# Turned gain columns, a four-head half tile, a shared room, a deeper expert ring and another merge order in a hybrid decoder step

## The reference

```
n1 = RMSNorm(x)*(1+scale1)+shift1 ;  h = n1 @ w_in        (1024 x 8704)
branch A: gated linear recurrence, 4 heads, 128x128 state, chunked; head norm * silu gate -> @ w_branch_a
branch B: dilated sliding-window attention, 3 groups x 4 heads x 128, merged by softmax denominators -> @ w_branch_b
x += gate1 * ((sigmoid(gA)*yA + sigmoid(gB)*yB) @ w_out)
n2 = RMSNorm(x)*(1+scale2)+shift2
PEER: q = n2 @ wq, 8 heads; per head two lists of 128 key scores, top 16 of each, top 16 of the 256 sums
      -> 16 experts of 16384; out += softmax * gelu(n2 . u[e]) * v[e];   x += gate2 * out
```

## Time and profile before

| | us |
|---|---|
| median of three runs | 4417.76 |
| the profiled execution | 4406.08 |
| its span, first to last instruction | 4404.3 |
| TensorE busy | 3094.3 (70%) |
| VectorE busy | 2596.8 (59%) |
| ScalarE busy | 1942.7 (44%) |
| GpSimd busy | 1497.0 (34%) |
| HBM traffic | 1455 MB, 330 GB/s over the span |

### The profile page before, as it was taken

One profiled execution on the slowest core, in us unless ns is written; L12 is line 12 of the kernel. 1 busy time (PEld: TensorE's weight loads), 2 busy tenths in 40 slices (PEclk: granted clock), 3 DMA queues, 4 the chain that ended last, 5 costly groups with the idle time before them and its releaser, 6 DMA issues. The chain is left out here.

```text
span 4404.3 us, 46846 instructions
## 1 busy us (share of the span) xinstructions
PE 3094.3 (70%) x14243; PEld 1672.3 (38%) x14243; DVE 2596.8 (59%) x6557; ACT 1942.7 (44%) x6708; POOL 1497.0 (34%) x1174
## 2 busy tenths in 40 slices
PE   7998868874999998575644686875555555555556
PEld 4677754741543456353432464551111111111111
DVE  2362334376568755684655545557767766766774
ACT  2122431045457844564442225445555545545554
POOL 4544102353322333222221112324444444444443
PEclk8999888977999999666876797886777777877778
DMA  6534244389999999877999888999999999999998
GB/s 259 200 131 138 74 152 168 120 324 356 389 368 367 422 421 405 288 305 291 375 342 364 348 305 312 357 348 383 416 410 420 421 401 413 415 400 413 417 403 336
DMA packets 315488, 1450.91 MB, mean 329 GB/s; under 512 B 44258, under 2 KB 105602, under 8 KB 166883
## 3 DMA queue, kind: packets, MB, share of 16 engines
q0 software_dynamic: 152064, 1107.36, 62.5%
q1 hardware_dynamic: 148802, 333.34, 21.5%
q10 hardware_dynamic: 14368, 7.21, 0.6%
HBM read 1380.40 MB, written 74.57 MB: 330 GB/s over the span
## 5 line engine op out<-in xcount | busy, mean ns | idle before, releaser
L3010 POOL DMA_INDIRECT uv_ring<-in_peer_uv,pick_idx x1024 | 1157.4, 1130 | 2240.9 <-PE expert_acc L3183 1954.4
L3183 PE MATMUL expert_acc<-uv_ring,diag 128*64 128x512 f32 (+1 forms) x3968 | 1102.6, 796 | 720.5 <-ACT diag L3148 689.2
L3106 DVE SCALAR_TENSOR_TENSOR uv_ring<-uv_ring,n_pairs 128x1024 f32<-128x1024 f32 x756 | 924.7, 1235 | 574.8 <-DMA uv_ring<-in_peer_uv,pick_idx 525.9
L3183 PEld LDWEIGHTS expert_acc<-uv_ring,diag 128*64 128x64 f32 (+1 forms) x3968 | 241.2, 155 | 1482.7 <-ACT diag L3148 1050.3
L3135 ACT ACTIVATE gelu_cube<-dots_now 128x2 f32<-128x2 f32 x528 | 105.8, 200 | 1001.8 <-DVE uv_ring L3106 920.2
L3106 DVE SCALAR_TENSOR_TENSOR uv_ring<-uv_ring,n_more 128x1024 f32<-128x1024 f32 x268 | 326.4, 1225 | 216.9 <-DMA uv_ring<-in_peer_uv,pick_idx 209.0
L3143 ACT ACTIVATE pick_weight<-gelu_tanh,pick_share 128x1 f32<-128x1 f32 x1056 | 350.8, 379 | 17.6
L955 PE MATMUL h_acc_q<-in_w_all_q,n_all_q 128*128 128x512 f32 x640 | 283.6, 597 | 0.7 <-issue 0.7
L3138 ACT ACTIVATE gelu_tanh<-gelu_cube,dots_now 128x1 f32<-128x1 f32 x1056 | 253.3, 287 | 16.2
L3140 ACT ACTIVATE pick_share<-dots_now,pick_prob 128x1 f32<-128x1 f32 x1056 | 245.4, 280 | 0.0
L952 PE MATMUL h_acc_q<-n_all_q,in_w_all_q 128*128 128x272 f32 x896 | 215.3, 398 | 10.2 <-DMA in_w_all_q<-in_w_in 10.2
(11 more groups left out here) (460 smaller groups left out, 4959.4 us busy)
## 6 DMA issues: line engine op xcount, KB each, us to landing
in_w_p<-in_w_in SPq DMA_DIRECT2D x34, 1024.0 KB, 7.3
in_w_all_q<-in_w_in SPq DMA_DIRECT2D x17, 2048.0 KB
ada_w<-in_w_ada SPq DMA_DIRECT2D x10, 2048.0 KB, 7.9
uv_ring<-in_peer_uv,pick_idx POOLq DMA_INDIRECT x1024
past_keys_q<-in_past_keys SPq DMA_DIRECT2D x16, 1024.0 KB
past_rows_q<-in_past_values SPq DMA_DIRECT2D x16, 1024.0 KB
score_pair<-scores SPq DMA_DIRECT2D x66, 128.0 KB
wq_raw_p<-in_peer_wq SPq DMA_DIRECT2D x16, 512.0 KB, 5.9
```

Of the source, the lines that this page charges most:

```text
L3010: pool.indirect_dma_start(self.rows_of(part, s), None, self.x["peer_uv"][0], bass.IndirectOffsetOnAxis(ap=self.idx[:, q % 2, 2 * half + s, ...
L3106: ins = dve.scalar_tensor_tensor(out=row, in0=row, scalar=1.0, in1=n2[:, s if tile < LAST_TILE else 0, :], op0=ALU.mult, op1=ALU.mult, acc ...
L3183: ins = pe.matmul(self.acc[s * w:(s + 1) * w, c, :], self.diag[:, of % DIAGS, t, 0:w], rows, start=first, stop=last)
```

## The change

Seven parts. (1) Opening: the norm weight and two bias rows come as 24 rows of 128 from ScalarE's queue and TensorE turns them, instead of three loads of single elements on SP's queue; the two first bias loads move to ScalarE's queue; the first projection weights are loaded ahead of the fourth adaLN block; four of the eight columns are scaled and split before the last gains. (2) SP's wait for the last weights at the end of the first projection moves to GpSimd's turn that uses them. (3) First half: four of eight `w_branch_a` products are computed in `merge_phase` into PSUM of their own. (4) Heads 4 to 7 of tile 0 become a four-head group (parts 32 to 63); its search is dealt three steps a turn over turns 22 to 29. (5) Second half: `SharedRoom` takes the sixth ring slot's room after part 119 and holds the inputs of recurrence and attention; the first loads of the next phase are issued in the phase before it, the last stores are waited for in the phase after it. Attention and sample updates get another order. (6) Merge, second half: three spread buffers, of which only the used part is cleared, filled two ahead; the tile merge goes into the middle of the sample steps. (7) The ring has seven slots from part 226 and ten from part 261.

```diff
         modulation.load(2)
+        in_weights.load(0)
         modulation.load(3)
-        modulation.load_bias(0)
-        modulation.load_bias(1)
-        with nc.allow_non_contiguous_dma("one weight and two biases for each column"):
-            sp.dma_start(weight_col[:], x["norm1_w"].rearrange("a (c p) -> p (a c)", p=P)).then_inc(weight_in, 16)
-            for j in range(2):
-                sp.dma_start(bias_cols[:, j, :], x["b_ada"][:, j * D:(j + 1) * D].rearrange("a (c p) -> p (a c)", p=P)).then_inc(weight_in, 16)
-        in_weights.load(0)
...
+        by_chunk = lambda row: row.rearrange("a (c p) -> (a c) p", p=P)
+        act.dma_start(gain_rows[0:DC, :], by_chunk(x["norm1_w"])).then_inc(weight_in, 16)
+        for j in range(2):
+            act.dma_start(gain_rows[(1 + j) * DC:(2 + j) * DC, :], by_chunk(x["b_ada"][:, j * D:(j + 1) * D])).then_inc(weight_in, 16)
+        for b in range(MOD_SLOTS):
+            modulation.load_bias(b, act)
         act.wait_ge(c_loaded, 32)
...
         for c in range(DC):
+            if c == HALF:
+                modulation.copy(MOD_FIRST - 1)
...
-            turn(n)
-            if n + 1 < MOD_FIRST:
-                modulation.product(n + 1)
-            fold(n)
+            if n == N - 1:
+                turn(n)
+                fold(n - 1)
+            modulation.product(n)
+            if n < N - 1:
+                turn(n)
+            if n != N - 2:
+                fold(n)
...
         gains(0)
         modulation.rows(2)
+        for c in range(HALF):
+            move(c)
         gains(1)
-        for c in range(DC):
-            dve.wait_ge(moved, c + 1)
...
 
 class OutWeights:
@@ -699,7 +736,7 @@
 
...
+        else:
+            pool.wait_ge(self.loaded_before[half], 16 * (self.before + k + 1))
...
+            if room is not None and n == len(blocks) - 1:
+                for s in range(SLOTS):
+                    sp.wait_ge(stored[s], stores_in(s, -(-(first[IN_QK // WB] - s) // SLOTS)))
+                beside.wait_summed(MORE_TO + 1)
+                room.gates_and_rows()
...
-            for half in range(2):
-                sp.wait_ge(raw_in[half], 16 * LOADED)
         for s in range(SLOTS):
...
+                room.first_queries()
+                sp.wait_ge(tile_done, N_P)
+                room.first_values()
             beside.sp(cost(n) * (0.2 if w == S_TOK else 0.4))
...
-            sp.wait_ge(state_stored[0], 16 * DEC_B // 2)
-            sp.wait_ge(state_stored[1], 16 * DEC_B // 2)
-            sp.wait_ge(final_stored, 16)
+            sp.dma_start(new_state_p[0, 0].rearrange("h k v -> k h v"), state[:, 0]).then_inc(room.final_stored, 16)
 
...
-                at_least(dve, update_s, b - 1)
-                nc.vector.tensor_scalar(v_one[b % 2], v_in[0:S_TOK, s, :], own_row[:, b:b + 1], None, ALU.mult).then_inc(s_ones, 1)
+                own_values(b + 1)
                 dve.wait_ge(update_s, b + 1)
-                at_least(dve, state_stored[b % 2], 16 * (b // 2))
...
+                if b < HEADS:
+                    sample_rows(b)
...
+            if s == 0:
+                sp.dma_start(self.reset, self.consts["chunk_reset"]).then_inc(self.tables_in, 16)
+                sp.dma_start(self.causal.rearrange("p a b -> p (a b)"), self.consts["chunk_causal"]).then_inc(self.tables_in, 16)
+            sp.dma_start(self.v_in[:, s], self.dram["h_r"][at:at + P, R_I:R_I + WIDTH]).then_inc(self.row_in[s], 16)
+            sp.dma_start(self.g_in[:, s], of_gate(T_G, at)).then_inc(self.row_in[s], 16)
+        sp.dma_start(self.masks.rearrange("p a b -> p (a b)"), self.consts["att_masks"]).then_inc(self.masks_in, 16)
+
...
-            load_keys(j + 2)
-            for i in of_job(j):
-                load_past(i + 2)
             sp.wait_ge(result_ready, j + 1)
             for at, dst in queries(dram["att"][g]):
                 sp.dma_start(dst, result[at, j % 2].rearrange("p h d -> p (h d)")).then_inc(stored[j % 2], 16)
             load_values(j + 2)
+            load_keys(j + 3)
+            for i in of_job(j):
+                load_past(i + 2)
             beside.sp(12.0)
...
+            at_least(dve, added, i - P_SLOTS + 1)
+            if i < P_SLOTS:
+                s_link(nc.vector.memset(p_one[i], 0.0))
+            else:
+                s_link(nc.vector.memset(spread(p_one[i % P_SLOTS], loads[i - P_SLOTS][1]), 0.0))
...
                 for i in range(n * PER, (n + 1) * PER):
-                    spread_probs(i)
+                    if i + P_SLOTS - 1 < len(loads):
+                        spread_probs(i + P_SLOTS - 1)
+                    if i % PER == PER // 2 - 1:
+                        merge(n + 1)
+                    if i % PER == PER // 2 and n:
+                        leave(n - 1)
...
+            if early is not None:
+                early.product(n)
             pe.wait_ge(merged_ready, n + 1)
...
             for j, o in enumerate((o_a, o_b)):
+                if j == 0 and m < begun:
+                    continue
...
-    HEADS_READ = {2: 4, 13: 6}
+    HEADS_READ = {2: 4, 20: 8}
...
-MORE_FROM, MORE_TO = 33, 125
+MORE_FROM, MORE_TO = 33, 119
+QUERY_FROM, QUERY_SLOTS = 226, 2
+TAIL_SLOTS = 3
 LEAD = 2
...
-AS_WRITTEN = (1,)
+AS_WRITTEN, FIRST_FOUR = (1,), 2
+FOUR_SCORES, FOUR_PICKS, FOUR_STEPS = 20, 22, 3
...
+    if tile == 0:
+        return ((0, 2), (2, 2), (4, 4))
+    return tuple((h, 2) for h in range(0, PH, 2))
+
...
+    tail_from = FRONT_PARTS + LEAD + QUERY_SLOTS
+    out = [(PART_SLOTS, MORE_FROM, MORE_TO)]
+    out += [(first + k, QUERY_FROM, N_PARTS) for k in range(QUERY_SLOTS)]
+    out += [(first + QUERY_SLOTS + k, tail_from, N_PARTS) for k in range(TAIL_SLOTS)]
+    return out
```

More of the change, by code:

```diff
@@ L2360, in query_phase @@
     C_S = 1.5
-    stores = [(4 if at // P in QUAD_TILES else 2) if w == P else 1 for _, w, at in tiles]
+    stores = lambda n, heads: sum(P // row_tokens(tiles[n][2] // P, h) if tiles[n][1] == P else 1 for h in range(heads))
     block = ph.block()
@@ L2976, in sp @@
                     self.load_scores(q, s)
[L2977 to L2978 removed]
+        for n, rows in enumerate(ROW_HALVES):
+            if n and i == rows.first - rows.half - (8 if rows.tile == 0 else 1 if rows.half and n >= ROW_SLOTS else 12):
                 self.load_n2(n)
@@ L3226 @@
 MOD_US = 250.0
-FRONT_PARTS = 257
 FRONT_US = 2140.87
@@ L3334, in front @@
                             if busy:
-                                later[0].more = held(rows, "uv_more", [P, 2, 2 * D])
-                            phase(project_phase, tag, busy, span, second, const, n_hi, n_lo, split_weights, ahead, x, consts, dram)
+                                later[0].more[PART_SLOTS] = room.room
+                            phase(project_phase, tag, busy, span, second, const, n_hi, n_lo, split_weights, ahead, x, consts, dram, room)
                             if busy:
```

413 lines of the change are left out of this document (287 added, 126 removed).

## The result

The changed kernel takes 4377.41 us (median of 5, 4363.64 to 4382.25) against 4417.76 (4412.14 to 4424.89): a ratio of 0.991, 95% interval 0.9893 to 0.9927. That is 40 us less; the forecast was 79 less. The profiled executions, 4375.05 against 4406.08 us, differ by 31.

> The changed kernel once more, as the run beside which the three others stand. All theories: ratio 0.991, between 0.989 and 0.993, stages within 3 us of its first profile, except the first half's, where the granted clock differs from run to run.

The account below looks back on a forecast made before the run. It took engines to bound the first half, TensorE and DMA the second projection, and bytes the experts alone. Terms summed to -87, -79 after bytes given back: 4327 us profiled, 4338 as median, 8-in-10 range 4292 to 4398.

Parts of the forecast that it names:

- opening: Start of the kernel up to the first projection: 6 us less (0 to 10).
- search in the first norm: Second half's first norm: tile 0's search puts more steps on VectorE there, 17 us more.
- second projection (sums, sixth slot): Second half's projection: tile 0's sums 17 us less (29 less to 0), losing the sixth slot earlier 2 more.
- recurrence (start, samples, end): Second recurrence: 14 us less at its start, 8 in its samples, 11 at its end.
- attention (start, order): Second half's attention: 5 us less at its start, 8 less by the order of loads.
- merge: Second half's merge: 6 us less (15 less to 0), with TensorE's wait for spread buffers 50.4 us before.
- seven slots, query: Query stage with seven ring slots: 13 us less (30 less to 0), from fewer waits for gathers.
- ten slots, experts alone: End of the kernel, where only experts run, with ten ring slots: 8 us less (34 less to 0).
- bytes given back: Recurrence to merge: a seventh of the 52 us saved comes back as waits for gathers, turning -87 into -79.
- more than forecast: Rival, chance 0.10: TensorE's 29 us come in full, query fills its 21, loads' order gives 20: -130, 4288 us.
- SP's queue as the place for a rival: Rival, chance 0.04: SP waits for part 119 ahead of the last stores, so the prefetch fails: -37, 4381 us.
- the DMA engines bind from 1095 on: Rival, chance 0.18: first half -18, search +19, sums 0, slot +2, recurrence -33, the rest 0: -30, 4388 us.

Follow-up runs that it names:

- the run without the rows: Changed kernel, but tile 1's second half takes its products with the gate's rows, its own norm rows not loaded (output wrong): 4362.4 us, 0.9871 of the kernel before.
- best5: Changed kernel with second row halves loaded two turns earlier and the room's loads two by two between the last stores: 4363.61 us, 0.9883 of the kernel before.
- the one by pairs: Changed kernel, but tile 0 works all its heads two by two as before, searches at one step a turn: 4376.28 us, 0.9899 of the kernel before.

## Why the forecast was half right

By the profiled executions, forecast and measured:

| step | forecast | measured |
|---|---|---|
| opening | -6 | -8.3 |
| end of the first projection | -7 | -7.2 |
| early branch products | -5 | -5.2 |
| other stages of the first half | +2 | +8.5 |
| search in the first norm | +17 | +17.7 |
| second projection (sums, sixth slot) | -15 | +1.7 |
| recurrence (start, samples, end) | -33 | -25.0 |
| attention (start, order) | -13 | -2.3 |
| merge | -6 | -0.1 |
| seven slots, query | -13 | +0.4 |
| ten slots, experts alone | -8 | -12.6 |
| bytes given back | +8 | (in the rows above) |
| branch, out, second norm | 0 | +1.4 |
| sum | -79 | -31 |

*First half.* The three terms held. The first move's copy took 4.00 us beside the split, as the forecast took it from the earlier trace rows, but the three behind it 0.42 each. GpSimd's last split instruction ran from 36.87 to 41.40: only one move lay beside it, since the weights, and with them the split, came earlier too. So the opening gave 8.3 and not 6. The 8.5 us elsewhere are 2.1 and 2.7 in recurrence and attention, where the granted clock was 0.79 and 0.93 for 0.81 and 0.96 (in later profiles of the same code these stages took 116.8 to 123.9 and 118.0 to 126.6 us, 118.6 and 120.4 before), and 3.6 in the query stage, where 2 were forecast.

*Search and sums.* 17.7 us against 17 forecast for the search. In the projection 15 us were to go and none did, and three sizes are behind it. The sums were taken at 17 us, as TensorE's 29 cut down by the DMA share of 0.99; between parts 32 and 64 they gave 34 (29 in the run without the rows). There the rival *more than forecast* was right: TensorE's time came in full. Two costs were not in the sum at all. The half tile makes five row halves out of three in tiles 0 and 1 (the first expectation above says four), with three row slots: a wait of 18.0 us at part 65, 16 us between parts 64 and 66, and 12 of the stage by the run without these rows. And the prefetch was counted at nothing in the projection: 12.5 us, by the run with the loads moved back. That the stage came out at 689.3 and so near the 687.6 before is luck: 34 won, 16 and 13 lost again, and 6 in pieces that no run takes apart, 2 of them forecast for the sixth slot. I had named SP's queue as the place for a rival (17 + 30 us), but had it wait for part 119. It was the issue of the loads itself, and their bytes.

*Recurrence.* The stage took 221.5 us where 213 were forecast. The start gave 15.4 us for 14 (first scan 13.1 us after the barrier for 28.4), and the end 8.3 for 11 (from the last product of the recurrence at 2015.2 to 2028.8 before, from 2005.6 to 2011.0 now). The samples are what was mis-sized: from the first scan to that product 204.4 us became 203.1, 1.3 us less for the 8 counted. The idle 11.2 us of the earlier trace rows at its end are gone from VectorE, and 17.86 us of TensorE's appear at attention's start, where I had counted 5 less. Taking away the wait, reordering the loads or keeping gathers back moved it again.

*Attention, merge, query.* This is the step that failed most: 32 us counted from idle shares of 0.05 to 0.08 in the earlier trace rows, by which a stage could shrink until its share was 1. They gave 2. The new kernel runs these stages at 0.96, 0.97 and 0.93 in the old length. The waits named in the earlier trace rows shrank as forecast and came back as waits for past values and query weights. What the forecast did not ask is where in the stage the idle share lies. In the attention it is one hole of 10 us, in which no gather is in flight since GpSimd waits for TensorE; the change left it there and made it 14. It can be closed: three versions ran the same stage in 267 to 271 us at a share of 0.99 to 1.00. So the 13 us were to be had, but not by the reordering that was to bring them. In the merge one gap could be named, 14.8 us for expert rows; with it gone the stage took 149.5 us once and 152.3 to 154.7 in five other versions, for 150 forecast. For the query stage no run settles what fills the share.

*Slots.* The two counted together, 21 us, gave 15. Most of it comes one way: two more parts (261 for 259) are fetched when the query stage ends, 10 us at 421 GB/s. The query stage took 269.3 us without the slots and 263.6 to 266.0 with them, so it owes them 3 to 6 us of the 13 forecast, which the rest of the change took back.

The rival *the DMA engines bind from 1095 on* had -30 in the profiled run and 4388; measured -31 and 4377 (the profiled run before was 11.7 under its median, the changed one 2.4 under). Its number is right, its reason is not shown, and that is luck. In the projection its *sums 0* was false (34 us won, as much lost elsewhere in the stage), in the attention the engines did not bind (nearly the same bytes passed in 267 us), and the 12.6 us of the experts alone, which it put at 0, made up for 6 less in the first half and 8 less in the recurrence. The rival *more than forecast* names 12, 8 and 12 us over the forecast's 87, which makes -119 and not -130.

Open: why the hole closes, and the attention takes 267 to 271 us, in three runs that changed only where the room's loads stand. A fourth of that kind, with the loads at the recurrence's start, kept the hole and took 284.3, and all others took 277 to 285. From 28 to 56 us after the stage's start the DMA share is 0.94 to 0.97 in the three and 0.47 to 0.71 in the seventeen other profiles. Fewer gathers in flight at the start was the theory; keeping them back did not bring it. It was not seen again in the combined versions: `best5` has the loads between the stores, leaves the attention as it is, and takes 280.7 us there.

## What to carry to other kernels

A wait with a name in the profile is worth its length only if nothing else is late next: ask for each wait removed which load the freed engine wants next, and when it is issued. A mean DMA share of 0.95 says neither that the stage is bound nor that 5% are free: cut the stage into short windows and look for the hole, and for what the engine that issues the gathers waits for in it. A prefetch has its price where it is issued: count the issuing queue's time and the bytes up to the barrier of the stage that hosts it. When a change adds a user of a small set of buffers (here a fifth row half on three slots), draw up who waits for which buffer at every border. And when a run undoes two things at once, as the one by pairs did, its difference is their sum: cut the stage at the work's own marks before giving it to one of them.

## What was not expected of the hardware

Issuing one load of the room took SP 0.4 to 10 us: the eleven loads of the recurrence's inputs held SP for 35 us in a stage with a DMA share of 0.99, for 28 us at the recurrence's start (1778.4 to 1806.4, the stage's share 0.80), and ScalarE for 20.8 us. A load of 32 rows issued at 2016.06 us held TensorE until 2041.97, some 26 us later, with gathers in front of it; in the run with the loads after the stores, issued at 2016.12, it was there before 2025.67.
